# Activations read already turned, their root applied at the evictions, and matmuls of ones at the start

## The reference

```python
h = jnp.concatenate([meta, x], axis=1)
hn = rmsnorm(h, ln_mix_w[l])          # h * rsqrt(mean(h*h) + eps) * weight
proj = hn @ w_in
q, k, v, g_out, g_low, z, xbc, dt_raw, gate_a, gate_b = split_cols(proj, IN_SPLITS)
log_g = jax.nn.log_sigmoid(g_low @ gla_w_gate2 + gla_b_gate) / GLA_GATE_NORM
```

## Time and profile before

| | |
|---|---|
| three runs | 1537.99, 1535.9, 1538.38 us (median 1537.99) |
| profiled execution | 1535.95 us, of which the span in the trace is 1534.1 us |
| first product matmul | 16.74 us from the span's start |
| gate matmuls | 32.05 us |
| first product of `g_out` | 70.21 us |
| first product behind them | 93.29 us |

### The profile page before, as it was taken

How to read it: one execution, slowest core, us unless ns; L and a number is a source line. 1 busy time by engine, 2 the same in 40 slices (tenths; PEclk the granted TensorE clock), 3 DMA queues, 4 the chain that set the end, 5 groups by cost and what they waited for, 6 DMA issues and landing times.

```text
span 1534.1 us, 17792 instructions
## 1 busy us (share of the span) xinstructions
PE 1369.2 (89%) x6585; PEld 984.2 (64%) x6585; DVE 1050.4 (68%) x2081; ACT 671.9 (44%) x1221; POOL 297.0 (19%) x265
## 2 busy tenths in 40 slices
PE   6999989999997987687877787778899999999997
PEld 6989979879996433233333333333497788998876
DVE  5867578776688776777677677665785466655554
ACT  5665677555463322122222222222453465645662
POOL 1000000000023654444544443442100000000000
PEclk9999999999998999989989998999999999999999
DMA  7454454545778999999999999999765456554442
GB/s 247 157 165 137 148 168 139 179 125 178 277 291 343 421 421 421 422 421 421 422 421 421 421 422 421 422 421 422 283 209 163 125 181 197 161 175 143 158 141 81
DMA packets 77797, 417.64 MB, mean 272 GB/s; under 512 B 8768, under 2 KB 8832, under 8 KB 44688
## 3 DMA queue, kind: packets, MB, share of 16 engines
q0 software_dynamic: 36864, 268.45, 42.3%
q1 hardware_dynamic: 40848, 148.06, 29.9%
HBM read 415.39 MB, written 1.08 MB: 271 GB/s over the span
## 4 chain that ended last, share of the span: by engine, by line
PE 54%; DMA 27%; DVE 11%; ACT 5%; issue 2%; POOL 1%; DVEq 0%; SPq 0%; POOLq 0%; ACTq 0%
DMA SLAB<-in_peer_uv,C 20%; PE ps L1025 13%; PE ps L1027 13%; PE ps L1026 12%; PE ps L1312 9%; DMA AR<-in_peer_uv,C 6%; DVE wlo L1898 2%; DVE SLAB L2215 1%; DVE AR L2215 1%; ACT whi L1478 1%; PE ps L1246 1%; DVE AR L2059 1%; POOL SLAB L2447 1%; PE ps L1231 0%; DMA AR<-scr 0%
## 5 line engine op out<-in xcount | busy, mean ns | idle before, releaser
L1898 DVE TENSOR_TENSOR wlo<-raw,whi 128x1024 fp32r<-128x1024 f32 x246 | 299.5, 1221 | 172.1 <-ACT whi L1478 171.4
L1478 ACT ACTIVATE whi<-raw 128x1024 fp32r<-128x1024 f32 x246 | 258.7, 1056 | 131.3 <-PE ps L1027 122.2
L1312 PE MATMUL ps<-SLAB,AR 128*128 128x512 f32 x516 | 253.9, 648 | 60.4 <-ACT AR L1686 60.0
L1312 PE MATMUL ps<-AR 128*128 128x512 f32 x508 | 246.3, 638 | 67.4 <-ACT AR L1686 66.1
L1025 PE MATMUL ps<-XH,whi 128*128 128x256 f32 (+1 forms) x1032 | 300.9, 292 | 4.4 <-DVE AR L2059 1.6
L1027 PE MATMUL ps<-XH,wlo 128*128 128x256 f32 (+1 forms) x1032 | 293.9, 285 | 0.0
L1026 PE MATMUL ps<-XL,whi 128*128 128x256 f32 (+1 forms) x1032 | 293.8, 285 | 0.0
L2447 POOL DMA_INDIRECT AR<-in_peer_uv,C x127 | 143.1, 1127 | 609.6 <-DVE C L1878 428.8
L1312 PEld LDWEIGHTS ps<-SLAB,AR 128*128 128x128 f32 x516 | 104.5, 207 | 206.3 <-issue 123.9
L1312 PEld LDWEIGHTS ps<-AR 128*128 128x128 f32 x508 | 100.6, 203 | 211.9 <-issue 115.5
L2215 DVE CUSTOM_DVE_ANT_0 SLAB<-SLAB,AR 128x1024 f32<-128x1024 f32 x129 | 157.0, 1224 | 74.2 <-DMA SLAB<-in_peer_uv,C 74.0
(11 more groups left out here) (374 smaller groups left out, 1456.6 us busy)
## 6 DMA issues: line engine op xcount, KB each, us to landing
raw<-in_stream SPq DMA_DIRECT2D x246, 512.0 KB, 3.7
AR<-scr SPq DMA_DIRECT2D x8, 512.0 KB, 5.4
AR<-in_stream SPq DMA_DIRECT2D x7, 512.0 KB, 8.2
SLAB<-in_peer_uv,C POOLq DMA_INDIRECT x129, 28.3
AR<-in_rows SPq DMA_DIRECT2D x4, 512.0 KB, 4.9
SLAB<-in_stream SPq DMA_DIRECT2D x4, 512.0 KB, 8.7
AR<-in_peer_uv,C POOLq DMA_INDIRECT x127, 28.2
AR<-in_con SPq DMA_DIRECT2D x1, 1280.0 KB, 7.1
```

Source lines behind the costliest of these rows:

```text
L1312: t = pe.matmul(ps[2 * i + half][:, :], d, rows_in[:, 512 * half:512 * half + 512], start=c == 0, stop=c == 127)
L1478: a.activation(whi[i % NS][:, :], src, ACT.Copy).then_inc(*hi.up(i))
L1898: v.tensor_tensor(wlo[i % NS][:, :], src, whi[i % NS][:, :].bitcast(F32), ALU.subtract).then_inc(*lo.up(i))
```

## The change

The host lays out a further input `xt`: for each of the eight feature blocks the 272 rows already turned, with the weight `ln_mix_w` ahead of them. The first 25 chunks (small, k, q, v and `g_out`) are computed from halves of the turned rows that carry the weight but not the root (`XH0`, `XL0`). The root is applied where products leave PSUM: k, q and small are multiplied by `RBX`, the root spread over all partitions, and that on VectorE (ScalarE evicted them before); g and the turned v take it as a scalar operand. `RBX` is made by three matmuls of ones with diagonals of the root (step `spread_x`), behind chunk 2. For all later products the turned rows are multiplied by `RBX` and halved again (step `rescaled_x`, eight times, spread over chunks 3 to 9). TensorE runs `WARMING` = 11 matmuls of ones at the start. Chunks 0 to 3 have their matmuls in another order, so that those with low halves come last. The loads are reordered. The gates' strand starts behind q1 instead of k3.

```diff
+WARMING = 11
+RESCALED_AT = {"k2": (0,), "k3": (1,), "q0": (2, 3), "q1": (4,), "q2": (5,), "q3": (6,), "v0": (7,)}
...
     yield say("begin")
-    for c in range(5):
...
+    yield from split(0)
+    for k in range(8):
+        yield say("raw_x", k)
+    yield from split(1)
+    yield from split(2)
+    yield say("x_roots")
...
+    unscaled = []
+
     def qkv(c, i, b):
-        yield say("qkv", c, i, b)
-        if c == "k3":
+        unscaled.append((c, i, b))
+        if c == "k1":
+            yield say("spread_x")
+        if c not in ("small", "k0"):
+            while unscaled:
+                yield say("qkv", *unscaled.pop(0))
+        for k in RESCALED_AT.get(c, ()):
+            yield say("rescaled_x", k)
+        if c == "q1":
             side(gates_side())
...
+                if step == "begin":
+                    on.wait_ge(*dve.of("ones"))
+                    for _ in range(WARMING):
+                        pe.matmul(ps[5][:, 0:128], ONES, ONES, start=True, stop=True)
+                elif step == "spread_x":
+                    on.wait_ge(*dve.of("x_diagonals"))
+                    pe.matmul(ps[4][:, 0:16], ONES[0:16, :], RD[0:16, 0:16], start=True, stop=True)
+                    for i in range(2):
+                        m = pe.matmul(ps[4][:, 16 + 128 * i:144 + 128 * i], ONES, RD[:, 16 + 128 * i:144 + 128 * i], start=True, stop=True)
+                    m.then_inc(*side.up("spread_x"))
...
                 elif step == "qkv":
                     c, i, b = at
-                    free[b] = act.of(c)
+                    free[b] = act.of(c) if c[0] == "v" else dve.of(c)
...
+                elif step == "raw_x":
+                    k, = at
+                    t = slice(k * T, k * T + T)
+                    on.wait_ge(s_xt[k // 4], 16)
+                    on.wait_ge(s_xt[0], 16)
+                    a.activation(XH0[:, t], XTK[:, k, :], ACT.Copy, scale=XT[:, k:k + 1]).then_inc(*act.up(("raw_x", k)))
...
+                elif step == "rescaled_x":
+                    k, = at
+                    on.wait_ge(*dve.of(("scaled_x", k)))
+                    a.activation(XH[:, k * T:k * T + T], XTK[:, k, :], ACT.Copy, scale=XT[:, k:k + 1]).then_inc(*act.up(("rescaled_x", k)))
...
-                    if c == "small":
-                        a.copy(SMT[:, :], ps[b][:, 0:T]).then_inc(*act.up(c))
-                    elif c[0] == "k":
-                        a.copy(kT[:, n, :], ps[b][:, 0:T]).then_inc(*act.up(c))
-                    elif c[0] == "q":
-                        a.mul(qT[:, n, :], ps[b][:, 0:TX], 128.0 ** -0.5).then_inc(*act.up(c))
...
+                elif step == "qkv":
+                    c, i, b = at
+                    n = int(c[1:]) if c != "small" else 0
+                    if c[0] != "v":
+                        on.wait_ge(*prod.of((i, 1)))
+                        on.wait_ge(*act.of("spread_x"))
+                        if c == "small":
+                            v.tensor_tensor(SMT, ps[b][:, 0:T], RBX, ALU.mult).then_inc(*dve.up(c))
+                        elif c[0] == "k":
+                            v.tensor_tensor(kT[:, n, :], ps[b][:, 0:T], RBX, ALU.mult).then_inc(*dve.up(c))
+                        else:
+                            v.scalar_tensor_tensor(qT[:, n, :], ps[b][:, 0:TX], 128.0 ** -0.5, RBX[:, NM:T], ALU.mult, ALU.mult).then_inc(*dve.up(c))
+                elif step == "rescaled_x":
+                    k, = at
+                    t = slice(k * T, k * T + T)
+                    on.wait_ge(*dve.of(("raw_x", k)))
+                    on.wait_ge(*act.of("spread_x"))
+                    v.tensor_tensor(XTK[:, k, :], XTK[:, k, :], RBX, ALU.mult).then_inc(*dve.up(("scaled_x", k)))
+                    on.wait_ge(*act.of(("rescaled_x", k)))
+                    v.scalar_tensor_tensor(XL[:, t], XTK[:, k, :], XT[:, k:k + 1], XH[:, t].bitcast(F32), ALU.mult,
+                                           ALU.subtract).then_inc(*dve.up(("rescaled_x", k)))
...
                 if step == "begin":
+                    half = 8 + 4 * T
+                    load(0)
+                    sp.dma_start(XT[:, 0:half], xt[:, 0:half]).then_inc(s_xt[0], 16)
+                    sp.dma_start(XT[:, half:8 + 8 * T], xt[:, half:8 + 8 * T]).then_inc(s_xt[1], 16)
+                    load(1)
                     sp.dma_start(HX[:, 0, :], x_tiles[:, 0, :]).then_inc(s_x0, 16)
+                    load(2)
                     sp.dma_start(HX[:, 1, :], x_tiles[:, 1, :]).then_inc(s_x1, 16)
...
                     sp.dma_start(HX[0:16, 2, :], meta).then_inc(s_meta, 16)
-                    sp.dma_start(C1[:, :], con1).then_inc(s_con1, 16)
-                    sp.dma_start(PAR[:, :], par).then_inc(s_con1, 16)
-                    for n in range(NR):
-                        load(n)
+                    sp.dma_start(C1[:, 0:128], con1[:, 0:128]).then_inc(s_con1, 16)
+                    load(3)
+                    sp.dma_start(PAR[:, :], par).then_inc(s_par, 16)
+                    sp.dma_start(C1[:, 128:NC1], con1[:, 128:NC1]).then_inc(s_par, 16)
```

More of the change, by code:

```diff
@@ L842, in order_of_work, with build @@
     yield say("sb_post")
-def build(nc, stream, par, rows, con1, con2, xin, meta, subk, peer_uv, out):
+def build(nc, stream, par, rows, con1, con2, xin, xt, meta, subk, peer_uv, out):
     ctx = ExitStack()
@@ L2419, in pool_program @@
             for step, *at in order_of_work():
[L2420 to L2428 removed]
+                if step == "gather":
                     m, j, before = at
@@ L2595, in lay_params, with lay_features @@
     return p
+def lay_features(inp):
+    both = np.concatenate([np.asarray(inp["meta_tokens"]), np.asarray(inp["x"])[0]], axis=0)
+    turned = both.T.reshape(8, 128, T).transpose(1, 0, 2).reshape(128, 8 * T)
+    return np.concatenate([columns(inp["ln_mix_w"]), turned], axis=1)
 def lay_rows(inp):
@@ L2639, in lay_out @@
         "xin": np.asarray(inp["x"])[0],
+        "xt": lay_features(inp),
         "meta": np.asarray(inp["meta_tokens"]),
```

139 lines of the change are left out of this document (73 added, 66 removed).

## The result

The changed kernel takes 1545.41 us (median of 6 runs, 1544.96 to 1546.62) against 1538.28 for the kernel before, measured beside it: 1.0047 times as long, 95% interval 1.0037 to 1.0058, so 7.1 us slower. The forecast was 1540.7 with a range up to 1544.5: the sign of the sum was right, its size too small, and the time lies outside the range. The profiled execution took 1545.25 us, with a span of 1543.4, which is 9.3 more than the 1534.1 of the earlier trace rows. The profiled execution of before was itself 2.3 us under its median, so of the 9.3 about 7 are the change.

The account below looks back on a forecast made before the run. VectorE's way from the gate matmuls to the low halves, not TensorE alone, was taken as the bound; chunk 17 coming 2.7 us later, with side steps at 0, gave 1537.99 + 2.7 = 1540.7 us, range 1535 to 1544.5.

Parts of the forecast that it names:

- Prologue, root, chunks 0 to 3: Start: products begin ten us sooner, near 6.5; root's spreading follows chunk 2 at 16.4; chunk 3 starts at 17.0, ends 20.0.
- Fifth 17.5: Loads at the start: the fifth weight tile lands at 17.5 us, with 406 KB/us dealt in issue order.
- My bound for late loads, 1.0: Start: tiles taking 5 us instead of 3.7 to land, or landing 1 us later, cost 1.0.
- Where the time goes at the start: Chunks 4 to 17: VectorE's evictions and rescalings delay the gate sums to 38.1; TensorE waits 5 us; chunk 17 2.7 later.
- The walk: Step-by-step timing of the start over VectorE, ScalarE and TensorE: gate sums 38.1, low half 13 57.3, chunk 17 72.6.
- The evictions on VectorE, 2.7 us: Ahead of the gate sums: seven evictions left on ScalarE would take 2.7 us out of VectorE's way, chunk 17 level with now.
- The ones, nothing: Start of TensorE: eleven matmuls of ones cost and bring nothing, since VectorE takes the gate matmuls' result only at 38.1.
- The side steps stand half a chunk later; I take 0: Behind chunk 17: decay, normalised rows and states stand 1.5 us later against the stream; taken as 0 since TensorE waits little.
- its bound of 1.5: Where TensorE waits for a side step, the later place adds between 0 and 1.5 us.
- The sum: Whole kernel: +2.7 us on 1537.99, giving 1540.7 us; on the profile, span 1536.8.
- the walk of before: Same walk through the earlier kernel's rows: chunk 14 at 60.7, chunk 17 at 69.9; trace has 61.01 and 70.21.
- lost further on: Rival behind chunk 17: half chunk costs full 1.5, or loads come a us late; +4 to +5, 1542.5; chance 0.38.

Follow-up runs that it names:

- the run with that edit alone: Kernel before with one edit, the gates' strand started behind q1 instead of k3: 1540.5 us, ratio 1.0012.
- the run with two pieces caught up: Changed kernel with two extra pieces of the side strands said behind chunk 20, gates still behind q1: 1544.4 us, ratio 1.0038.
- the late constants: Changed kernel with the loads of the parameters and the rest of the constants issued behind the seventh tile: 1543.79 us, ratio 1.0036.
- the fastest repair: Changed kernel, rescaling products on GpSimd, constants behind seventh tile, own bank for chunk 0, gates behind q1, two extra side pieces behind chunk 20: 1534.81 us.

## Why the prediction failed, step by step

- **Prologue, root, chunks 0 to 3: right.** First product 6.36 (said 6.5), chunk 3 at 17.40 (17.0), the spreading at 16.61 (16.4).
- **"Fifth 17.5": the step that failed first.** The bytes were there at 17.4; the tile counted as landed near 19.6. I had dealt bytes in order and given no load more than its bytes; the last packets had no term. Everything behind it carries the 2.1 to 2.3 us: gate sums at 40.19 (38.1), low half 13 done at 59.5 (57.3), chunk 17 at 74.85 (72.6). My bound for late loads, 1.0, was half of it. What makes the last packets late is open for the greater part.
- **Where the time goes at the start: right.** Chunk 4 waited for "small" on VectorE, a rescaling held VectorE 1.4 us and the next low half 0.45 more (said 0.57), TensorE waited 4.1 us ahead of chunk 13 (said 5), and the way over VectorE set chunk 17. The runs with another bank, with rescalings in g and with GpSimd show this by three sides. The walk had no clock in it: chunk 4 took 4.61 us instead of 3.03 behind its wait, which VectorE's lateness hid.
- **The evictions on VectorE, 2.7 us: right** (3.0 by the medians, 2.1 at chunk 17, with the root left out).
- **The ones, nothing: right**, for the reason given. The wait ahead of chunk 4 took up the half pace: without the ones it was 1.46 us instead of 4.33, in part because chunk 4 itself came 1.3 us sooner there.
- **"The side steps stand half a chunk later; I take 0": the second step that failed**, and its bound of 1.5 with it. I read the earlier trace rows, one wait of 2.5 us, as little to wait for. It was the longest line of seven, and the nine waits of that stretch made 9.2 us already. With the side steps two pieces later against the stream they became thirteen and 14.1 us, 4.9 more. By the table above the strand's place costs 3.8 to 4.8 us in the traces (2.2, with 0.3 to 3.4 as its interval, by the medians of the run with that edit alone); the run with two pieces caught up shows that the place of the steps is what costs it. Why just these steps then collide with products is not shown; the longest new waits are for banks that the convolution's steps on VectorE free late.
- **The sum.** +2.7 said, +7.1 measured, 4.4 missing. Chunk 17 came 4.64 later in the trace, 1.9 more than said (the tail's 2.2, less the 0.3 by which the walk of before was short). The strand's place, put at nothing, is +4.4 in the traces and +2.2 by the medians, and 1.9 and 2.2 are near the 4.4. Which part of before's profiled execution is 2.3 us faster than its median is not known.
- **A rival that was near:** "lost further on" had both mechanisms, but priced them at 1.5 and 1. Its 1542.5 was made of sizes that no row bounded, and its full 5.2 us over now (2.7, 1.5 and 1) would still have been short.

## What to carry to other kernels

A start that comes ten us sooner is worth what the engine behind it can follow: walk the busiest side engine, count each wait inside a pair of steps that two engines pass to and fro, and give such work to an idle engine or to a later stage with room, never to a stage that is merely less full. When a strand of side work is moved by two chunks, all that is said behind it moves against the stream too: sum up the waits of the whole stretch, not the longest line, and look at its last consumer as well as its first. Where a load is moved back in a queue, ask which tile still stands behind it: the late constants gave chunk 4 three us, and over half of them were lost again at the eighth tile. And a tile has landed when its last packet has, here up to two us behind the bulk of its bytes, and not in every execution.

## What was not expected of the hardware

**The clock falls behind a wait.** Chunk 4 of the changed kernel, behind its wait of 4.3 us (the granted clock is the third number from the end of a row):

```profile
25.00:27.00 2.00, 2.00 (x12) 2.00 (x13) 2.00 (x5) 0.00 (x0) 0.00 (x0) 0.72 0.92 336
27.00:29.60 2.60, 2.60 (x14) 2.60 (x13) 1.56 (x4) 1.47 (x2) 0.00 (x0) 0.56 0.83 265
```

TensorE starts at full pace, 0.125 us from matmul to matmul, and from 25.98 to 29.15 goes at 1.2 GHz, 0.227 apart. The chunk takes 4.61 us instead of 3.03, and chunk 13 behind its wait 4.64. The waits of 4.3 and 4.1 us thus cost 5.9 and 5.8 us of TensorE's time. The slow pace cost nothing here, because VectorE was late anyway. In the run with two pieces caught up TensorE was the bound, and there the clock behind the wait of 1.97 us cost 1.7 more; in the fastest repair it stayed at 1.00 behind a wait of 2.0.

**GpSimd beside VectorE.** Eight products on GpSimd took 10.22 us, 0.77 to 1.76 each. Beside them VectorE's low halves took longer, its evictions from PSUM did not:

```profile
23.93 10.22 POOL L2490 TENSOR_TENSOR AR<-AR 128x272 f32<-128x272 f32 x8 [23.48 <-ACT AR L1516]
```
```profile
28.10 1.79 DVE L1969 TENSOR_TENSOR wlo<-raw,whi 128x1024 fp32r<-128x1024 f32 x1
29.88 0.44 DVE L1956 TENSOR_TENSOR AR<-ps,AR 128x272 f32<-128x272 f32 x1
```

1.79 us instead of 1.23, 0.44 as ever. The Trainium skill (SBUF — State Buffer, SBUF: two separate sides) says that the two engines share a pair of ports, as a lock, for VectorE's instructions with two inputs in SBUF; an eviction has one of its inputs in PSUM. This trace agrees in which of VectorE's instructions grew, and the spread of GpSimd's own times fits a lock that both sides pay for. It was cheap enough here: 5.3 us were won.
